# Two residual blocks on one core: the order of the regions in SBUF

## The reference

```python
# first block
h = rms_norm(x, mix_norm_g)
p = h @ w_in
y = concatenate([y_lru, y_ml, y_mo])        # three mixers on slices of p
x = x + y @ w_out
x = x + memory_cross_attention(rms_norm(x, xa_norm_g), rms_norm(mem, mem_norm_g), xa_wq, xa_wkv, xa_wo)
x = rms_norm(x, final_norm_g)
# second block
h = rms_norm_2(x, g_pre)
proj = h @ w_in_2
y_a, y_b, y_c, y_m = ...                     # pooling, windowed attention, gated linear attention, memory attention
gates = sigmoid(g_logits.reshape(B, S, 4, D) + b_merge)
merged = (gates[:, :, 0] * (y_a @ w_br_pool) + gates[:, :, 1] * (y_b @ w_br_swa)
          + gates[:, :, 2] * (y_c @ w_br_gla) + gates[:, :, 3] * (y_m @ w_br_mem))
x = x + rms_norm_2(merged @ w_out, g_post)
```

## Time and profile before

| what | before |
|---|---|
| runs | 3206.68 us median of 3 (3204.28 to 3206.87) |
| profiled execution | 3204.43 us, span 3202.5 us, granted clock 0.999 |
| TensorE, matmuls (PE) | 3188.2 us, 100% of the span |
| TensorE, weight loads (PEld) | 2664.3 us, 83% |
| VectorE / ScalarE / GpSimd | 1341.0 / 1290.5 / 1063.5 us |
| DMA | 364.49 MB, mean 114 GB/s |

### The profile page before, as it was taken

The page is one execution under the profiler, slowest core; times in us unless marked ns, Lnnn a source line. Parts: engine busy times, 40 slices in busy tenths (PEclk is TensorE's granted clock), DMA queues, the critical chain, the costliest instruction groups (busy, mean ns, idle before and its releaser), DMA issues.

```text
span 3202.5 us, 41942 instructions
## 1 busy us (share of the span) xinstructions
PE 3188.2 (100%) x15426; PEld 2664.3 (83%) x15426; DVE 1341.0 (42%) x1885; ACT 1290.5 (40%) x1992; POOL 1063.5 (33%) x460
## 2 busy tenths in 40 slices
PE   9999999999999999999999999999999999999999
PEld 8877888888888888888888888888888888888887
DVE  3573321113123534401111111144369999999802
ACT  6543322333235534332323323422345555555532
POOL 7633333433443434443433443344430000000043
PEclk9999999999999999999999999999999999999999
DMA  8622323233433423243333323433544444444442
GB/s 290 180 79 66 86 66 86 79 85 99 121 107 100 142 74 93 83 132 102 87 85 92 91 80 92 137 100 92 156 130 136 137 137 139 131 136 133 143 152 99
DMA packets 546539, 364.49 MB, mean 114 GB/s; under 512 B 18808, under 2 KB 505208, under 8 KB 545144
## 3 DMA queue, kind: packets, MB, share of 16 engines
q1 hardware_dynamic: 522912, 321.50, 35.4%
q10 hardware_dynamic: 23512, 41.40, 3.7%
HBM read 333.49 MB, written 29.36 MB: 113 GB/s over the span
## 4 chain that ended last, share of the span: by engine, by line
PE 98%; DVE 1%; ACT 1%; issue 0%; POOL 0%; DVEq 0%; ACTq 0%; POOLq 0%
PE proj L785 59%; PE s L1555 6%; PE t L1555 6%; PE s L1558 3%; PE t L1558 3%; PE s L1601 3%; PE proj L1601 1%; PE s L1255 1%; PE t L1601 1%; PE t L810 1%; PE proj L1555 1%; PE s L854 1%; PE s L847 1%; PE t L1255 1%; PE proj L1255 1%; PE t L854 1%
## 5 line engine op out<-in xcount | busy, mean ns | idle before, releaser
L756 POOL TENSOR_TENSOR w_lo<-raw,w_hi 128x1024 fp32r<-128x1024 f32 x431 | 1061.4, 2477 | 2113.1 <-ACT w_hi L1638 2086.1
L785 PE MATMUL proj<-ht_hi,w_hi 128*128 128x512 f32 x2400 | 955.6, 398 | 0.0
L785 PE MATMUL proj<-ht_hi,w_lo 128*128 128x512 f32 x2400 | 935.5, 390 | 0.0
L785 PE MATMUL proj<-ht_lo,w_hi 128*128 128x512 f32 x2400 | 934.5, 389 | 0.0
L1638 ACT ACTIVATE w_hi<-raw 128x1024 fp32r<-128x1024 f32 x396 | 404.4, 1053 | 385.8 <-PE proj L785 223.3
L785 PEld LDWEIGHTS proj<-ht_hi,w_hi 128*128 128x128 f32 x2400 | 451.0, 188 | 95.0 <-issue 4.8
L785 PEld LDWEIGHTS proj<-ht_hi,w_lo 128*128 128x128 f32 x2400 | 450.5, 188 | 95.5
L785 PEld LDWEIGHTS proj<-ht_lo,w_hi 128*128 128x128 f32 x2400 | 451.0, 188 | 94.8 <-issue 4.7
L3594 DVE TENSOR_TENSOR w_lo<-raw,w_hi 128x1024 fp32r<-128x1024 f32 x128 | 156.1, 1219 | 16.5 <-ACT w_hi L2508 15.5
L2512 ACT ACTIVATE w_hi<-t_w 128x1024 fp32r<-128x1024 f32 x96 | 101.9, 1062 | 105.9 <-DVE t_w L3612 53.3
L3594 DVE TENSOR_TENSOR w_lo<-t_w,w_hi 128x1024 fp32r<-128x1024 f32 x96 | 116.9, 1218 | 12.8 <-ACT w_hi L2512 12.8
(11 more groups left out here) (693 smaller groups left out, 4949.1 us busy)
## 6 DMA issues: line engine op xcount, KB each, us to landing
raw<-in_w_in_dram SPq DMA_DIRECT2D x404, 512.0 KB, 3.8
raw<-in_w_out_dram SPq DMA_DIRECT2D x64, 512.0 KB, 3.9
g_zt<-z_spill SPq DMA_DIRECT2D x64, 256.0 KB, 3.9
raw<-in_xa_wkv_dram SPq DMA_DIRECT2D x16, 512.0 KB, 7.2
raw<-in_w_mem_kv_dram SPq DMA_DIRECT2D x16, 512.0 KB, 3.7
raw<-in_w_br_gla_dram SPq DMA_DIRECT2D x16, 512.0 KB, 4.0
z_spill<-z_early ACTq DMA_DIRECT2D x32, 256.0 KB, 3.1
raw<-in_w_br_pool_dram SPq DMA_DIRECT2D x16, 512.0 KB, 4.2
```

Source lines behind the costliest of these rows:

```text
L756: pool.tensor_tensor(w_lo[:, slot, :], raw[:, slot, :], w_hi[:, slot, :].bitcast(F32), ALU.subtract).then_inc(lo_done, 1)
L785: ins = pe.matmul(dst, w, x[:, kt, c0:c1], start=first and n == 0 and m == 0, stop=last and n == len(kts) - 1 and m == 2)
```

## The change

The order of the calls that lay out SBUF. The two rings of rounded weights go from the first place to behind `xy`, `raw` goes behind them, and `kv1` and `kv2` go ahead of `xy`. Nothing else differs: each engine has the same instructions in the same order, on other addresses (and the lines of the file behind the place are one lower). `dist` and all that follows it stay where they were.

```diff
-        w_hi = keep("w_hi", [P, RING, HALF], F32R)
-        w_lo = keep("w_lo", [P, RING, HALF], F32R)
-
         ht_hi_at, ht_lo_at = take(KT * T * 4), take(KT * T * 4)
         ht_hi = at("ht_hi", [P, KT, T], ht_hi_at, F32R)
         ht_lo = at("ht_lo", [P, KT, T], ht_lo_at, F32R)
         m_at = take(M_REGION)
         m_end = m_at + M_REGION
-        raw = keep("raw", [P, RING, HALF])
-        xy_at = take(KT * T * 4)
-        xy = at("xy", [P, KT, T], xy_at)
         kv1_at = take(8192)
         k1, v1 = at("k1", [P, 4, M], kv1_at), at("v1", [P, 4, 2, P], kv1_at + 4096)
         kv2_at = take(8192)
         k2, v2 = at("k2", [P, 4, M], kv2_at), at("v2", [P, 4, 2, P], kv2_at + 4096)
+        xy_at = take(KT * T * 4)
+        xy = at("xy", [P, KT, T], xy_at)
+        w_hi = keep("w_hi", [P, RING, HALF], F32R)
+        w_lo = keep("w_lo", [P, RING, HALF], F32R)
+        raw = keep("raw", [P, RING, HALF])
```

## The result

The changed kernel takes 3221.23 us (median of 5 runs, 3219.48 to 3222.75), the kernel before 3205.86 us in the runs beside it. The ratio is 1.0050, with a 95% interval of 1.0039 to 1.0061: 15.4 us slower, between 12.5 and 19.6. The forecast was 3230 us, +23.1, with a range of 3205 to 3246.

A forecast was written before the change was run, and what follows sets the result against it. TensorE, busy 3188.2 of 3202.5 us, was taken to bound the kernel; 17.5 + 7.5 + 0.6 − 2.5 = +23.1 us on 3206.7 gave 3229.8, some 3230 us, with a range of 3205 to 3246.

The forecast's parts named there:

- Line 785 on `ht`, `yh`, `yl`: 7968 projection matmuls go from difference 0 to 448, 2.2 ns dearer each: +17.5 us, ends 0 and +53.
- Weights moving: Lines 1255 and 1601, 1152 matmuls at 233.3 ns for 226.8: +7.5 us; line 847, 192 matmuls: +0.6 us.
- `yp`: Pooling branch's product, 384 matmuls: the difference becomes 0, 226.7 for 233.3 ns each, −2.5 us.
- Gates' products: Six of seven kinds go from difference 0 to 448, `s4x` from 64 to 0: 0, ends −8 and +5 us.
- `o`: 192 matmuls on `o_hi`/`o_lo` go from difference 448 to 384: 0, ends ±1 us.
- Other engines: ScalarE, GpSimd, VectorE and DMAs meet the rings or `raw` at other addresses: no cost.
- the first and the fourth term: Line 785 on `ht`, `yh`, `yl`, foreseen at +17.5 us, and the gates' products, foreseen at 0.
- no address counts: Rival: start addresses do not matter, `yp` is slow for what runs beside it; time stays 3206.7 us; chance 0.11.
- only the moving operand: Rival: only the moving operand's start counts, so only the moving weights get dearer, +8.1 us, 3214.8 us; chance 0.07.
- any difference costs 6.6 ns: Rival: every difference but 0 costs 6.6 ns, making line 785's term 53 us, total 3265 us; chance 0.07.
- Off the common start is cheaper: Rival: shifted stationary weights make line 785's matmuls 5 ns cheaper, −40 us, total 3172 us; chance 0.04.
- the first rival: The rival that no start address counts, by the rule of two independent ports: 3206.7 us, chance 0.11.

The follow-up runs named there:

- e1: Changed kernel with the 1088-byte parameter table laid ahead of the rings, which start at remainder 0 by 512 again; 3204.38 us, ratio 1.0001.
- e2: Kernel before, old order, with the parameter table put between rings and activations, so ht_hi, ht_lo and m_at start at 64; 3220.15 us, ratio 1.0051.
- e5: Changed kernel with 1344 bytes of small tables ahead of the rings, which start at 256 by 512; 3203.55 us, ratio 1.0000.
- e6: Changed kernel with the parameter table and 32 free bytes ahead of the rings, which start at 32 by 512; 3260.56 us, ratio 1.0180.
- e7: Changed kernel with tables ahead of and between the rings, so w_hi starts at 0 and w_lo at 64; 3236.53 us, ratio 1.0105.

## Why the prediction was right

The finding it rested on holds: one form of matmul has several step lengths, and the difference of the two starts tells which. e1 and e2 make it more than a fit: the same loss is taken back and brought about by 64 bytes within 512, once on the stationary and once on the moving side. One part of it was wrong without harm to the sum: the difference counts within 256 bytes, not 512 (e5). Term by term, against the stages:

- *Line 785 on `ht`, `yh`, `yl`: +17.5 foreseen.* The two stages together gained 6.2 + 8.5 = 14.7 us, `o` included. The steady step was hit (229.0 ns, +2.3). The mean over all, 14.2/7968 = 1.8 ns, was lower than the 2.2 taken; by groups the price is uneven, (962.9 − 955.6)/2400 = 3.0 ns on `ht_hi` by `w_hi`, 2.1 on `ht_hi` by `w_lo` and 0.7 on `ht_lo` by `w_hi`, 1.9 on average. The lower bound from the means, 1.2, pointed that way. The term was mis-sized because it took the steady step: over all steps on `ht` (those over 300 ns left out) the trace's starts give 227.2 ns before and 229.1 after. So the uneven steps lift the mean by 0.5 ns over the steady step before the change and by 0.1 after it; why is not shown.
- *Weights moving: +8.1.* Lines 1255 and 1601 gave 2.5 + 5.0 = 7.5 us for 7.5. The 0.6 us of line 847 cannot be told from the first stage's own wait.
- *`yp`: −2.5.* −2.5 us.
- *Gates' products: 0, ends −8 and +5.* −3.6 us. This is one step that was mis-sized, and it had no row. By the trace's starts, the six products that went from 0 to 448 lost 0.5 us at 512 columns and gained 4.0 us at 256 (276 ns on `s2x` for 282); on `s4x` the two sides cancelled as foreseen, −1.15 and +1.09 us.
- *`o`: 0.* 25.3/64 against 25.1/64, +3 ns on `o_hi` by `w_lo`, a third of it; about +0.5 us if the rest does the same.
- *Other engines: nothing.* VectorE's split has 1219 and 1217 ns after, and the gates' stage got no longer for it.

Without the first stage's 2.0 us the profiled sum is +16.2 us, next to the +15.4 of the medians; the forecast was 7 us above, by the first and the fourth term, 3 to 4 us each. Of the rivals, *no address counts* fell with `yp` at 226.7 ns, *only the moving operand* with the 229.0 ns on `yh`/`yl`, whose own start stayed, and with e1, and *any difference costs 6.6 ns* with the 229.0 ns at 448, though e6 shows that at most differences it is near the truth. *Off the common start is cheaper* showed clearly in one place alone, the products' 256 columns.

The Trainium skill's rule of two independent read ports (TensorE: Matmul & The Clock Gate, "Step-by-step: what each phase is for") read as the first rival reads it, that no start address counts, does not agree with these runs: with the rings' start at the remainder 448 the stream of matmuls has 229.0 ns, at 0 (e1) it has 226.7. Whether it is the two reads that meet is not shown.

## What to carry to other kernels

Where TensorE bounds a kernel, look at the step between two starts of one form of matmul, operand by operand; two lengths for one form are a question with an answer. In a layout made by hand, give the stationary and the moving operands of float32r matmuls of 512 columns starts that are equal modulo 256 bytes, and check it whenever a table of an odd size is put ahead of them; 64 bytes were worth 0.5%, 32 bytes 1.8%. The rule is not for matmuls of 256 columns: the gates' stage, half of them, was 3.6 us quicker off the common start. Before believing that an order of regions is better or worse, pad it so that the remainders stay, and see whether anything is left.

## What the runs showed that was not expected

The price goes by the difference modulo 256 bytes, not 512: 226.7 ns at 0 (and 256), 233.3 at 32, 64 (and 320) and −32, 234.2 at 96, 232.5 to 233.3 at 128, 229.0 at 192 (and 448), all for runs of 512 columns of float32r at full clock. It is not symmetric, and no run of such steps tried lies under 226.7. Which part of the chip makes it so (the two operands' reads meeting in some way is a guess that the period fits) was not tried apart and stays open. And a step depends on what ran before it, so that mixtures are not means: e7 cost 33 us for the 10.5 worked out from its parts.
